# Order of the steps inside an attention unit, and GpSimd memsets, in a two-layer hybrid decoder

## What is computed

```python
def _masked_softmax(s, mask):
    s = jnp.where(mask, s, -jnp.inf)
    m = jnp.max(s, axis=-1, keepdims=True)
    p = jnp.exp(s - m)
    return p / jnp.maximum(jnp.sum(p, axis=-1, keepdims=True), 1e-30)
# prompt attention, for each head and branch: scores, softmax, values
s = jnp.einsum('btgrd,bngd->btgrn', qg, k_c) * (HEAD_DIM ** -0.5)
p = _masked_softmax(s, mask)
o = jnp.einsum('btgrn,bngd->btgrd', p, v_c)
# gated delta rule, for each chunk
A = eye + jnp.where(strict, jnp.einsum('bihd,bjhd->bhij', kb, kc) * L, 0.0)
Tinv = lax.linalg.triangular_solve(A, eye, left_side=True, lower=True)
u = jnp.einsum('bhij,bjhe->bihe', Tinv, vc * bc[..., None])
S = (S * jnp.exp(G_last)[..., None, None]
     + jnp.einsum('bjhd,bjhe->bhde', kc * jnp.exp(G_last[:, None] - G)[..., None], v_new))
```

## Time and profile before

| | |
|---|---|
| median of 3 runs | 2518.5 us (2511.68 to 2520.64) |
| the profiled execution | 2515.68 us, its span 2514.1 us |
| TensorE (PE) busy | 2198.9 us, 87% of the span |
| VectorE (DVE) busy | 1259.0 us, 50% |
| ScalarE (ACT) busy | 805.4 us, 32% |
| GpSimd (POOL) busy | 418.5 us, 17% |
| `delta_attention`, first layer | from 368.2 to 720.3 us of the span |
| `delta_attention`, second layer | from 1616.9 to 1969.3 us |

### The profile page before, as it was taken

How to read it: one execution, slowest core, us unless ns; L and a number is a source line. 1 busy time by engine, 2 the same in 40 slices (tenths; PEclk the granted TensorE clock), 3 DMA queues, 4 the chain that set the end, 5 groups by cost and what they waited for, 6 DMA issues and landing times. The chain is left out here.

```text
span 2514.1 us, 36111 instructions
## 1 busy us (share of the span) xinstructions
PE 2198.9 (87%) x12280; PEld 1625.6 (65%) x12280; DVE 1259.0 (50%) x2982; ACT 805.4 (32%) x1678; POOL 418.5 (17%) x648
## 2 busy tenths in 40 slices
PE   6999868888889999997979997688788799999977
PEld 3644447667767887886346444477677588888853
DVE  2244364566536666654122534545664366666532
ACT  2211112334334444441222211133343345445402
POOL 0110001001133333420001100010111333344100
PEclk9999867889869999995979997688888799999969
DMA  4452100000066877862044521000000768678431
GB/s 180 161 193 67 46 22 2 1 10 1 1 152 161 185 175 155 189 128 82 32 146 161 184 67 37 23 1 1 10 1 2 176 164 182 159 177 185 101 113 38
DMA packets 173056, 243.10 MB, mean 97 GB/s; under 512 B 50714, under 2 KB 132282, under 8 KB 172192
## 3 DMA queue, kind: packets, MB, share of 16 engines
q1 hardware_dynamic: 143328, 147.27, 23.0%
q0 software_dynamic: 29536, 93.43, 14.4%
HBM read 223.69 MB, written 25.50 MB: 99 GB/s over the span
## 5 line engine op out<-in xcount | busy, mean ns | idle before, releaser
L609 PE MATMUL bank<-W,hT 128*128 128x512 f32 (+3 forms) x1152 | 447.7, 540 | 14.2 <-DMA W<-in_w_in 10.1
L609 PEld LDWEIGHTS bank<-W,hT 128*128 128x128 f32 x1152 | 216.6, 194 | 203.4 <-issue 172.1
L978 PE MATMUL bank<-XT,W 128*128 128x256 f32 (+1 forms) x768 | 250.8, 462 | 0.0
L1035 POOL DMA_DIRECT2D SHARED<-in_cache_nsa_kv x256 | 152.1, 594 | 454.0 <-DVE RP L948 353.9
L1219 POOL TENSOR_TENSOR work<-UP,SHARED 128x512 f32<-128x512 f32 x56 | 72.2, 1293 | 877.0 <-DVE UP L1504 518.5
L967 ACT ACTIVATE XT<-bank 128x512 f32<-128x512 f32 x256 | 140.1, 593 | 125.6 <-PE bank L960 124.7
L1035 POOL DMA_DIRECT2D PS<-in_cache_nsa_kv x256 | 150.7, 589 | 138.7 <-issue 126.5
L1428 DVE TENSOR_REDUCE mx<-bank 128x1 f32<-128x31 f32 (+4 forms) x192 | 75.0, 390 | 196.5 <-PE bank L1287 193.3
L978 PEld LDWEIGHTS bank<-XT,W 128*128 128x128 f32 x768 | 135.0, 190 | 49.6 <-issue 36.9
L960 PE MATMUL bank<-CF,RP 128*128 128x128 f32 x1024 | 146.2, 289 | 9.2 <-DVE RP L948 8.8
L1247 ACT ACTIVATE Pr<-bank,mx 128x31 f32<-128x31 f32 (+4 forms) x192 | 85.7, 446 | 210.3 <-DVE mx L1429 210.0
(11 more groups left out here) (395 smaller groups left out, 3732.8 us busy)
## 6 DMA issues: line engine op xcount, KB each, us to landing
SHARED<-in_cache_nsa_kv SPq DMA_DIRECT2D x256, 128.0 KB, 5.7
SHARED<-in_cache_nsa_kv POOLq DMA_DIRECT2D x256, 128.0 KB, 5.5
PS<-in_cache_nsa_kv SPq DMA_DIRECT2D x256, 128.0 KB, 6.2
PS<-in_cache_nsa_kv POOLq DMA_DIRECT2D x256, 128.0 KB, 5.8
W<-in_w_in SPq DMA_DIRECT2D x48, 512.0 KB, 3.8
XS<-scratch_conv_p POOLq DMA_DIRECT2D x24, 384.0 KB, 4.5
PW<-in_state_nsa_win SPq DMA_DIRECT2D x16, 512.0 KB, 3.8
Wo<-in_w_out SPq DMA_DIRECT2D x4, 2048.0 KB, 11.9
```

The lines of the kernel that those rows point to most:

```text
L609: return nc.tensor.matmul(bk((c * NTILE + t) % BANKS)[:, 0:b - a], hT[:, k, t * P:(t + 1) * P], W[:, k // 2, k % 2, 0:b - a], start=(k == ...
L978: mm = nc_(self.v).tensor.matmul(out, self.v['W1'][:, kv, s, :], seg[:, s], start=(s == 0), stop=(s == SEG // PAIRS - 1))
L1035: e.dma_start(where[side * HD:(side + 1) * HD, slot, :, :], A['cache_nsa_kv'][l, page].rearrange("(p r) a g d -> p r (a g d)", r=PAIRS)[:, ...
```

## The change

Three edits. TensorE's walk of a unit becomes S(x), V(x-2), T(x-1). ScalarE's walk becomes E(x), the `OB` copy if due, C(x-1). The memsets at the head of `retention` and `delta_attention` go from VectorE's queue to GpSimd's, and whoever waited for them waits for GpSimd.

```diff
@@ delta_attention, ScalarE @@
             def unit(u):
 
+                if u < NU:
+                    qt, br, h = units[u]
+                    n = keys(u)
+                    e.wait_ge(shift, u + 1)
+                    if u >= DEEP:
+                        e.wait_ge(turned, u - DEEP + 1)
+                    nc.scalar.activation(Pr[:, u % DEEP, 0:n], sbank(u)[:, 0:n], ACT.Exp, scale=SCALE, bias=mx[:, u % DEEP, 1:2],
+                                         accum_out=SUM[:, u // GROUP % 2, h % 2, br:br + 1]).then_inc(exped, 1)
                 if u >= 2 and (u - 2) % GROUP == GROUP - 1:
                     k = (u - 2) // GROUP
                     e.wait_ge(used, u - 1)
...
                     nc.scalar.activation(PT[0:m, (u - 1) % 2, 0:k, :], bk(TURN, 4)[0:m, 0:k, :], ACT.Copy).then_inc(copied, 1)
-                if u < NU:
...
-                    nc.scalar.activation(Pr[:, u % DEEP, 0:n], sbank(u)[:, 0:n], ACT.Exp, scale=SCALE, bias=mx[:, u % DEEP, 1:2],
-                                         accum_out=SUM[:, u // GROUP % 2, h % 2, br:br + 1]).then_inc(exped, 1)
@@ delta_attention, TensorE @@
                 if what == "unit":
+                    if x < NU:
+                        scores(x)
                     if x >= 2:
                         values(x - 2)
                     if 1 <= x <= NU:
                         turn(x - 1)
-                    if x < NU:
-                        scores(x)
                     continue
@@ delta_attention, GpSimd and VectorE @@
         @block.gpsimd
         def _(e):
+            pool.done(e, "z1", nc.gpsimd.memset(S[:, :, :], 0.0))
+            pool.done(e, "z2", nc.gpsimd.memset(SS[:, :, :, :], 0.0))
...
         @block.vector
         def _(e):
-            dve.link(e, "z1", nc.vector.memset(S[:, :, :], 0.0))
-            dve.link(e, "z2", nc.vector.memset(SS[:, :, :, :], 0.0))
             e.wait_ge(gl, 16)
@@ retention @@
+        @block.gpsimd
+        def _(e):
+            pool.done(e, "z3", nc.gpsimd.memset(W2[:, :, :, :], 0.0))
+            pool.done(e, "z1", nc.gpsimd.memset(S[:, :, :], 0.0))
+            pool.done(e, "z4", nc.gpsimd.memset(HS[:, :, :], 0.0))
+            pool.done(e, "z5", nc.gpsimd.memset(KCG[:, :, :], 0.0))
+            pool.done(e, "z2", nc.gpsimd.memset(SS[:, :, :, :], 0.0))
...
         @block.vector
         def _(e):
-            dve.link(e, "z3", nc.vector.memset(W2[:, :, :, :], 0.0))
-            dve.done(e, "z4", nc.vector.memset(HS[:, :, :], 0.0))
-            dve.done(e, "z5", nc.vector.memset(KCG[:, :, :], 0.0))
-            dve.link(e, "z1", nc.vector.memset(S[:, :, :], 0.0))
-            dve.link(e, "z2", nc.vector.memset(SS[:, :, :, :], 0.0))
             e.wait_ge(gl, 16)
```

More of the change, by code:

```diff
@@ L700, in retention @@
     cp.HALVES, cp.SECOND = (5, 5), (6, 7)
-    dn = ["z3", "z4", "z5", "z1", "z2"]
+    dn = []
     pn, an = [], []
@@ L722, in retention @@
     dn += ["kc0", "kc1"]
-    with stage(["dve_s", "act_s", "pe_s", "loaded", "gl", "rows", "small", "outs"]) as \
-            (block, (dve_s, act_s, pe_s, loaded, gl, rows, small, outs)):
+    with stage(["dve_s", "act_s", "pe_s", "loaded", "gl", "rows", "small", "outs", "cleared"]) as \
+            (block, (dve_s, act_s, pe_s, loaded, gl, rows, small, outs, cleared)):
         dve = Steps(dve_s, dn)
         act = Steps(act_s, an)
+        pool = Steps(cleared, ["z3", "z1", "z4", "z5", "z2"])
         pe = Steps(pe_s, pn)
@@ L733, in _ @@
                 e.dma_start(PG[:, i, :, :], O['kv_prompt'][l, 0].rearrange("(t p r) a g d -> t p r (a g d)", p=P, r=PAIRS)[i, :, :, 0:256]).then_inc(rows, 16)
-            dve.wait(e, "z3")
+            pool.wait(e, "z3")
             for kv in range(2):
@@ L742, in _ @@
             e.dma_start(v['B1'][:, :], A['cmp_b1'][l].rearrange("k e -> e k"), allow_slow_non_contiguous=True).then_inc(small, 16)
-            dve.wait(e, "z2")
+            pool.wait(e, "z2")
             load_states(e, SS, A['state_ret'], loaded, l)
@@ L809, in _ @@
                 if t < 4:
-                    dve.wait(e, "z1")
+                    pool.wait(e, "z1")
                     for hp in range(2):
@@ L881, in _ @@
                 if what == "back":
+                    if i == 0:
+                        pool.wait(e, "z2")
                     pe.wait(e, f"su{t}")
@@ L1130, in delta_attention @@
     TT_, ATT_, NTt_ = ([heads(t, i) for t in range(NTILE)] for i in range(3))
-    dn, pn, an = ["z1", "z2"], [], []
+    dn, pn, an = [], [], []
     ends = {}
@@ L1186, in delta_attention @@
         dve, act, pe = Steps(dve_s, dn), Steps(act_s, an), Steps(pe_s, pn)
-        pool = Steps(masked, [f"nn{t}.{k}" for t, k in steps])
+        pool = Steps(masked, ["z1", "z2"] + [f"nn{t}.{k}" for t, k in steps])
         @block.sync
@@ L1310, in values @@
                 mm.then_inc(used, 1)
-            before = "z2"
+            before = None
             for what, x in ORDER:
                 if what == "unit":
+                    if x < NU:
+                        scores(x)
                     if x >= 2:
@@ L1350, in _ @@
                 tri, same = cf('tri', P)[0:n, k, 0:n], cf('same', P)[0:n, k, 0:n]
-                if what in PRODUCTS or (what, t) == ("norm0", 4):
+                if before and (what in PRODUCTS or (what, t) == ("norm0", 4)):
                     dve.wait(e, before)
@@ L1373, in _ @@
                     if t < 4:
-                        dve.wait(e, f"s1{t-1}" if t else "z1")
+                        if t:
+                            dve.wait(e, f"s1{t-1}")
+                        else:
+                            pool.wait(e, "z1")
                         for hp in range(2):
@@ L1509, in _ @@
                 if what == "state0":
+                    if t == 0:
+                        pool.wait(e, "z2")
                     pe.wait(e, f"ks{t}")
```

## The result

The changed kernel takes 2493.4 us (median of 6 runs, 2490.47 to 2505.67) against 2517.8 us (2511.68 to 2520.64) in the same session. The ratio is 0.9915, with a 95% interval of 0.9894 to 0.9936. It is faster by 24 us by the medians, 21 by the ratio; I had forecast 51.

What follows compares the result with a forecast made beforehand. TensorE, the fullest engine in the delta stages, idled 61.2 us in a layer, mostly for the exponential. Waits 12, clock 12 and memsets 0.25, times 2, take 48.5 from 2515.7, giving 2467 us; range 2410 to 2500.

Steps and rivals of the forecast that it cites:

- What bounds the kernel: Delta stages: TensorE is fullest yet idles 61.2 us in a layer, 26.9 of it waiting for the exponential before the transposes.
- the 10 that I named: Delta stage: TensorE's wait for the exponential at T was to fall from 26.9 to under 10 us in a layer.
- The order of the unit: Attention units in the delta stages: T(x-1) and S(x) trade places, which was to save 18 us of waits in a layer.
- The idle time goes to about nothing: Long units: a need of 2.5 us from S(x) to V(x-1), filled by 2.45 us of TensorE work.
- 5.8 go: Short units, 480 to 560 us: of 11.0 us of waits in 15 pieces, 5.2 stay and 5.8 go.
- The case that I called slower: Delta stages, VectorE late: TensorE needs copy, V and T after the exponential, 0.8 us later each wait; 2545 us, chance 0.08.
- What is late next: Delta steps after long stretches, with VectorE's OB wait of 1 to 2 us in 16 places: 4 us lost in a layer.
- The table loads: ScalarE at the delta rule's square roots: copy now behind table load and exponential, 2 us lost in a layer, bound 6.4.
- The clock: Delta stages: fewer gaps raise TensorE's granted clock from 0.83 to near 0.9, saving 12 us in a layer.
- The memsets: Start of retention: VectorE's first copy released earlier, gain 0 to 0.5 us in a layer, taken as 0.25; nothing in delta.
- The sum: Both layers: 12 us of waits, 12 of clock and 0.25 of memsets, times 2, make 48.5 us saved.
- the lower of my two bounds: GpSimd memset of 2048 elements: 1.76 us as on VectorE at the low end, 5.2 us at the upper.

Runs made afterwards that it cites:

- `OB` ahead again: Changed kernel with ScalarE's OB copy moved back ahead of the exponential (OB, E(x), C(x-1)): 2462.3 us, ratio 0.9787 to the kernel before.
- ScalarE's whole walk put back: Changed kernel with ScalarE's old order restored, keeping TensorE's edit and the GpSimd memsets: 2433.7 us, ratio 0.9688 to the kernel before.
- scores first alone: Kernel before with only TensorE's walk changed to S(x), V(x-2), T(x-1): 2424.2 us against 2512.8, ratio 0.964; run again, 2427.4 us.
- exponential first: Kernel before with only ScalarE's walk changed to E(x), OB, C(x-1): 2637.9 us, ratio 1.0503.
- memsets alone: Kernel before with only the memsets moved to GpSimd, both walks as before: 2516.0 us against 2512.8, ratio 1.0006.
- before with late scaling: Kernel before with only VectorE's scaling of six units moved one unit later: 2523.0 us against 2516.2, ratio 1.0028.
- changed with late scaling: Changed kernel with VectorE's scaling of six units moved one unit later, behind the next maximum: 2466.0 us, ratio 0.9809 to the kernel before.

## Why the prediction was wrong

**What bounds the kernel.** Right: the edits act in the two delta stages, and TensorE's wait for the exponential was the one that ended last. It fell from 26.9 to 0.6 us, below the 10 that I named.

**The order of the unit.** This step failed, and with it the 18 us that it put into the sum: "The idle time goes to about nothing" for long units, "5.8 go" for short ones, 18 us saved in a layer. Idle time fell by 3.3 us in one layer and grew by 2.2 in the other. I had set the need from the end of S(x) at 1.85 + 0.60 + 0.05 us, and that holds only if VectorE is free when the scores end. I took this from its 60 waits before 96 maxima. But those 60 waits were made by the late scores of the old order. With scores a unit earlier, VectorE waits before 34, and in most of the others it comes from its own queued work or from the `OB` wait, after the scores have ended. So the exponential is late by VectorE's queue, and C stands behind it: V's waits for the copy, which I had left at 9.7 us, are 38.5. From 480 to 560 us, the stretch from which I had priced the short units, V's waits are 14.3 us in 13 pieces where T's were 11.1 in 15 and V's 1.2 in 4.

**The case that I called slower** was the mechanism, at work in part: after a late exponential TensorE needs copy, V and T before it gets on. I gave it 0.08 and asked whether it would outweigh the gain, when it had to be subtracted. Its price is the step from `OB` ahead again to ScalarE's whole walk put back: 29 us, about 14 in a layer. With neither copy behind the exponential, the run with scores first alone gains 44 to 47 us in each delta stage, not 13 to 16; its profile is of the fastest of six executions, and in the three other profiles of that order with the scaling in place the gain is 43 to 51.

**What is late next.** The wait for `OB` was foreseen as 1 to 2 us in 16 places and counted inside 4 us. It is 25.3 us in 16 places, and its part of the result is 31 us, 15 in a layer. I had laid it to V(x-2) behind S(x). With scores first alone, where V(x-2) also stands behind S(x), the wait is 9.1 us against 4.4 before, so this cause is worth about 5. With the `OB` copy ahead again it is 11.4. The larger cause is that the `OB` copy itself stands behind the exponential, a part of the diff that I priced nowhere. The growth of the delta chain's waits did not happen.

**The table loads.** I took 2 us in a layer. No run parts this from the rest of ScalarE's order, but the traces bound it. The waits of T and V that end within 2.5 us behind one of the ten table loads sum to 7.2 and 6.3 us in the two layers before, and to 8.3 and 7.6 in the changed kernel. They grew by about 1 us in a layer, so the loss lies elsewhere.

**The clock.** Right in size: 12 us in a layer forecast, busy time down by 12.5 and 15.0. It came with no less idle time, though, so my reason, fewer gaps, was not it, and the hit is luck. The rise lies outside the scatter that the profiles show: the six delta stages profiled with both walks as before have 285.6 to 299.0 us of busy time, the two of the changed kernel 278.4 and 280.0. What made it rise stays open.

**The memsets.** Right. VectorE's first copy in retention starts 3.0 us after TensorE's first instruction (296.76 against 293.74), and it is the gain vector that releases it. Before, it was 3.4. The gain is within the 0 to 0.5 us given. That the first retention stage is 2.1 us shorter is no gain of the memsets: the kernel with scores first alone, which has them on VectorE, shows such a stage as well, 69.6 us in its second layer.

**The sum.** -2 to 3 us for the waits and 12.5 to 15 for TensorE's busy time make 13 to 16 us in a layer, not 24. The range of 2410 to 2500 held the result, but by the clock and not by the waits. The forecast missed in its size: it was twice what came, and nearly all that it put on the waits is missing.

## What to carry to other kernels

Idle time of an engine before an instruction says who is late in the present order, not how much room the engine has once its input comes early; count its queued work up to that instruction as well. On an in-order engine, don't put an instruction whose input is ready ahead of time behind one that waits for a busy third engine, if a second engine needs the first. A diff with several edits can hold one that gives 89 us and one that costs 60: price each against the others, and run each alone. The prices need not add up either: the same ScalarE edit cost 125 us by itself and about 60 beside TensorE's.

## What the runs showed of the hardware

The GpSimd memset is about as fast as VectorE's. Timeline of the changed kernel at the start of retention:

```profile
294.17 0.30 POOL L759 MEMSET S<- 128x256 f32 x1
...
294.59 1.79 POOL L762 MEMSET SS<- 128x2048 f32 x1
```

2048 elements in 1.79 us against 1.76 on VectorE, the lower of my two bounds; the upper one, from the product of two inputs, was three times too high.

The granted clock goes with TensorE's idle time only in the rough. In first delta stages it was 0.74 with 96.9 of 418.4 us idle (exponential first) and 0.89 with 40.6 of 308.3 (scores first). Between these the order is loose (same stage of the other kernels): 65.7 of 351.3 at 0.84 (memsets alone), 61.2 of 352.1 at 0.83 (before), 57.9 of 356.9 at 0.80 (before with late scaling), 57.9 of 336.3 at 0.86 (changed), 52.0 of 323.2 at 0.87 (`OB` ahead again), 50.6 of 333.3 at 0.84 (changed with late scaling). Inside one stage it is no closer: in the kernel before, TensorE idled 11.8 us from 560 to 640 at a clock of 0.97, and 12.1 us from 640 to 720 at 0.73. So the total of idle time doesn't tell the clock, and what else does is not shown here.

Where the waits shrank much, the busy time shrank with them. From before to scores first the idle time fell by 20.7 us and the busy time by 23.1 in the first layer, by 14.4 and 32.7 in the second.
